# Sine and cosine tables made beside a projection, and a head's two decay spreads in different rows of the array

## What is computed

```python
# S5: 64 groups of 16 channels, 64 complex states each
lam_bar = exp(lam * dt)                    # one complex number per state
bu = einsum('gpc,bsgc->bsgp', b_bar, u_g)
states = scan(s -> lam_bar * s + bu)
y = einsum('gcp,bsgp->bsgc', c_mat, states).real + d * u
# SSD, per head, in chunks of 128 positions
dt = softplus(dt_raw + dt_bias); adt = dt * -exp(a_log)
acs = cumsum(adt)                          # within a chunk
lmat = exp(where(tri, acs[l] - acs[s], -inf))
y = (C B^T * lmat) @ (x * dt) + exp(acs) * (C @ carried_state)
```

## Time and profile before

| | |
|---|---|
| median of 3 runs | 3925.47 us (3924.04 to 3925.93) |
| the profiled execution | 3926.31 us, its span 3924.5 us |
| busy share of the span: PE, PEld, DVE, ACT, POOL | 93%, 73%, 53%, 28%, 28% |
| mean granted PE clock | 0.959 of 2.4 GHz |
| S5 stage | about 692 to 889 us |
| GLU | from 889 us |
| first, second SSD stage | about 2580 to 2641, 3305 to 3364 us |

### The profile page before, as it was taken

The page is one execution under the profiler, slowest core; times in us unless marked ns, Lnnn a source line. Parts: engine busy times, 40 slices in busy tenths (PEclk is TensorE's granted clock), DMA queues, the critical chain, the costliest instruction groups (busy, mean ns, idle before and its releaser), DMA issues. The chain is left out here.

```text
span 3924.5 us, 44371 instructions
## 1 busy us (share of the span) xinstructions
PE 3649.6 (93%) x16819; PEld 2845.9 (73%) x16819; DVE 2065.8 (53%) x2631; ACT 1080.3 (28%) x1480; POOL 1096.8 (28%) x835
## 2 busy tenths in 40 slices
PE   7999999878999979999899999987899999789999
PEld 6767888657788858887667888753688877257887
DVE  4556555894544475454555545655533346554334
ACT  4542221032212122212542221333321223332221
POOL 0635542700645236340544543012100000130000
PEclk9999999889999989999999999987999998899999
DMA  3215443033444334432214443200133321013332
GB/s 105 65 49 135 122 136 105 27 71 93 129 131 135 87 93 135 130 106 83 54 46 123 130 131 104 75 13 22 57 97 103 88 80 45 22 44 86 91 96 81
DMA packets 554319, 346.08 MB, mean 88 GB/s; under 512 B 33270, under 2 KB 535420, under 8 KB 554172
## 3 DMA queue, kind: packets, MB, share of 16 engines
q1 hardware_dynamic: 540348, 293.79, 26.6%
q0 software_dynamic: 13824, 50.34, 4.4%
HBM read 341.01 MB, written 3.08 MB: 88 GB/s over the span
## 5 line engine op out<-in xcount | busy, mean ns | idle before, releaser
L1273 PE MATMUL ps<-h_hi,w_hi 128*128 128x512 f32 x2880 | 1144.6, 397 | 41.6 <-DVE w_lo L1235 14.6
L1274 PE MATMUL ps<-h_lo,w_hi 128*128 128x512 f32 x2880 | 1127.4, 391 | 0.0
L1275 PE MATMUL ps<-h_hi,w_lo 128*128 128x512 f32 x2880 | 1126.2, 391 | 0.0
L1235 DVE TENSOR_TENSOR w_lo<-w,w_hi 128x2048 fp32r<-128x2048 f32 (+2 forms) x294 | 664.3, 2260 | 133.8 <-ACT w_hi L1228 131.7
L1228 ACT ACTIVATE w_hi<-w 128x2048 fp32r<-128x2048 f32 (+2 forms) x294 | 507.0, 1725 | 711.9 <-PE ps L1275 638.1
L1273 PEld LDWEIGHTS ps<-h_hi,w_hi 128*128 128x128 f32 x2880 | 545.1, 189 | 161.9 <-issue 36.1
L1275 PEld LDWEIGHTS ps<-h_hi,w_lo 128*128 128x128 f32 x2880 | 543.9, 189 | 115.2
L1274 PEld LDWEIGHTS ps<-h_lo,w_hi 128*128 128x128 f32 x2880 | 544.8, 189 | 107.9 <-issue 0.5
L1364 DVE TENSOR_TENSOR sg<-sg,ps 128x512 f32<-128x512 f32 x132 | 90.8, 688 | 719.2 <-ACT sg L1349 719.2
L1273 PE MATMUL ps<-a_hi,w_hi 128*128 128x512 f32 x1056 | 411.9, 390 | 0.0
L1275 PE MATMUL ps<-a_hi,w_lo 128*128 128x512 f32 x1056 | 411.0, 389 | 0.0
(11 more groups left out here) (471 smaller groups left out, 3971.6 us busy)
## 6 DMA issues: line engine op xcount, KB each, us to landing
w<-in_ffn_w_gate_up SPq DMA_DIRECT2D x176, 512.0 KB
w<-in_w_ada POOLq DMA_DIRECT2D x96, 512.0 KB, 6.9
w<-in_ffn_w_down SPq DMA_DIRECT2D x64, 704.0 KB
w<-in_w_gate_up SPq DMA_DIRECT2D x88, 512.0 KB
w<-in_w_down SPq DMA_DIRECT2D x32, 704.0 KB
w<-in_fox_w_in SPq DMA_DIRECT2D x32, 512.0 KB
w<-in_w_in SPq DMA_DIRECT2D x14, 1024.0 KB
w<-in_fox_w_in SPq DMA_DIRECT2D x8, 1024.0 KB
```

The lines of the kernel that those rows point to most:

```text
L1235: last = nc.vector.tensor_tensor(lo, raw, hi.bitcast(F32), ALU.subtract)
L1273: nc.tensor.matmul(out, hi, a[0][:, k, :], start=k == 0, stop=False)
L1274: nc.tensor.matmul(out, hi, a[1][:, k, :], start=False, stop=False)
L1275: return nc.tensor.matmul(out, lo, a[0][:, k, :], start=False, stop=k == kt - 1)
```

## The change

It takes the tables out of the S5 stage and puts them, as a side of its own, `S5Tables`, into the second half of layer 0's last projection, spread over chunks 0 to 6; the doubling of the angle after the last table is gone. `ec`, `es` move to arena tiles 8 to 15 and what stood there to 16 to 23. In SSD the small tensors get a second copy of the 8 rows in partitions 32 to 39 (`MR` = 40, which makes the rows between live too); the second spread reads these. `heads` is loaded five times over.

```diff
+MR = 32 + MH
-        self.s5_low = at("s5_low", 16 * S, [P, DK, S], F32R)
+        self.s5_low = at("s5_low", 8 * S, [P, DK, S], F32R)
-        self.heads = sb("heads", [MH, 4])
+        self.heads = sb("heads", [MR, 4])
...
-        self.ut = at(8, 4096).rearrange("p (g a c) -> p g a c", a=4, c=C5)
+        self.ut = at(16, 4096).rearrange("p (g a c) -> p g a c", a=4, c=C5)
...
-        self.ec, self.es = at(16, 2048), at(20, 2048)
+        self.ec, self.es = tables.ec, tables.es
...
         weights(0)
         for q in range(3):
             block(q)
         weights(1)
-        turns()
-        for n in (1, 2, 4, 8):
-            table(n)
         weights(2)
-        table(16)
         block(3)
         block(4)
         block(5)
         keep(0)
-        table(32)
         block(6)
...
+class S5Tables:
+    def __init__(self, m, prep):
+        self.m, self.sm = m, prep.sm
+        flat = m.arena[:, :]
+        self.ec, self.es = (flat[:, t * S:(t + 4) * S] for t in (8, 12))
+        self.etmp = flat[:, 0:1024]
...
+    def vector(self, e, j):
...
+        def cosines(n):
+            t = three(self.etmp[:, 0:32 * n], n)
+            wc, ws = wide(sm["cs"], n), wide(sm["sn"], n)
+            do(tt(ec[:, :, n:2 * n], ec[:, :, 0:n], wc, ALU.mult))
+            do(tt(t, es[:, :, 0:n], ws, ALU.mult))
+            do(tt(ec[:, :, n:2 * n], ec[:, :, n:2 * n], t, ALU.subtract))
...
+        def double():
+            do(tt(sm["t"], sm["cs"], sm["cs"], ALU.mult))
+            do(tt(sm["k"], sm["sn"], sm["sn"], ALU.mult))
+            do(stt(sm["sn"], sm["sn"], 2.0, sm["cs"], ALU.mult, ALU.mult))
+            do(tt(sm["cs"], sm["t"], sm["k"], ALU.subtract))
+        if j == 0:
+            for x in range(3):
+                double()
+                do(tt(sm["er"], sm["er"], sm["er"], ALU.mult))
+            nc.vector.memset(ec[:, :, 0:1], 1.0)
+            do(nc.vector.memset(es[:, :, 0:1], 0.0))
+        for n in {1: (1, 2), 2: (4,), 3: (8,), 4: (16,)}.get(j, ()):
+            cosines(n)
+            sines(n)
+            double()
+        if j == 5:
+            cosines(32)
+        if j == 6:
+            sines(32)
...
                 for i, name in enumerate(("dt_bias_2", "a_log_2")):
-                    e.dma_start(m.heads[0:MH, 2 * l + i:2 * l + i + 1], d[name][l].rearrange("(h a) -> h a", a=1)).then_inc(ld.sem, 16)
+                    for a in range(MR // MH):
+                        e.dma_start(m.heads[a * MH:a * MH + MH, 2 * l + i:2 * l + i + 1], d[name][l].rearrange("(h a) -> h a", a=1)).then_inc(ld.sem, 16)
...
-            mm(ps[:, b, :], m.ones[0:MH, :], self.am[h % 2], start=True, stop=True).then_inc(m.sem["bc_ready"], 1)
-            mm(ps[:, b + 1, :], m.ones[0:MH, :], self.am[h % 2], start=True, stop=False)
+            mm(ps[:, b, :], m.ones[0:MH, :], self.am[h % 2][0:MH], start=True, stop=True).then_inc(m.sem["bc_ready"], 1)
+            mm(ps[:, b + 1, :], m.ones[32:MR, :], self.am[h % 2][32:MR], start=True, stop=False)
...
-            ts(self.am[h % 2], self.acs, m.c("ident")[0:MH, h:h + 1], None, ALU.mult).then_inc(m.sem["am_ready"], 1)
+            ts(self.am[h % 2], self.acs, m.c("sel")[0:MR, h:h + 1], -1.0, ALU.mult, ALU.mult).then_inc(m.sem["am_ready"], 1)
...
-               units=l * 2 * (FH_K + 1), side=prep if l == 0 else None, final=l == 3)
+               units=l * 2 * (FH_K + 1), sides=(prep, tables) if l == 0 else (None, None), final=l == 3)
```

More of the change, by code:

```diff
@@ L731, with __init__ @@
     late = True
-    def __init__(self, m, w, norm, prep):
+    def __init__(self, m, w, norm, prep, tables):
         super().__init__(m)
@@ L740, in __init__ @@
         self.ug = at(0, 4096).rearrange("p (g c) -> p g c", c=S5_CH)
[L741 to L745 removed]
+        self.ut = at(16, 4096).rearrange("p (g a c) -> p g a c", a=4, c=C5)
+        self.y = [at(16 + 2 * i, 1024)[0:S5_CH].rearrange("p (j n) -> p j n", j=S5_L) for i in range(2)]
+        self.st = [[at(20 + i, 256, 256 * a).rearrange("p (r c) -> p r c", r=4) for a in range(2)] for i in range(2)]
+        self.rot = [at(22, 256, 256 * i) for i in range(4)]
+        self.ec, self.es = tables.ec, tables.es
         self.wt = [at(24 + i, S) for i in range(3)]
@@ L1011, in keep @@
             last.then_inc(m.sem["k_ready"], 1)
[L1013 to L1038, removed]
         weights(0)
@@ L1532, in end, with sync, tensor, scalar @@
         finish(self.m, c_loaded=32, s5_loaded=16 * 5, s5_rows=1, turned=1, s5_step=2, s5_act=2, c_turned=2, ct_ready5=2)
+class S5Tables:
[4 more added lines that the diff above has]
+        self.etmp = flat[:, 0:1024]
+    def sync(self, e): pass
+    def tensor(self, e, j): pass
+    def scalar(self, e, j): pass
+    def end(self): pass
+    def vector(self, e, j):
+        m, nc, sm = self.m, self.m.nc, self.sm
+        tt, stt = nc.vector.tensor_tensor, nc.vector.scalar_tensor_tensor
+        do = lambda ins: m.dve(e, ins)
+        three = lambda a, n: a.rearrange("p (i a) -> p i a", a=n)
+        wide = lambda a, n: a.rearrange("p (i a) -> p i a", a=1).broadcast_to([P, 32, n])
+        ec, es = three(self.ec, S5_CH), three(self.es, S5_CH)
+        def cosines(n):
[4 more added lines that the diff above has]
+            do(tt(ec[:, :, n:2 * n], ec[:, :, n:2 * n], t, ALU.subtract))
+        def sines(n):
+            t = three(self.etmp[:, 0:32 * n], n)
+            wc, ws = wide(sm["cs"], n), wide(sm["sn"], n)
+            do(tt(es[:, :, n:2 * n], es[:, :, 0:n], wc, ALU.mult))
+            do(tt(t, ec[:, :, 0:n], ws, ALU.mult))
+            do(tt(es[:, :, n:2 * n], es[:, :, n:2 * n], t, ALU.add))
+        def double():
[17 more added lines that the diff above has]
+            sines(32)
 class SplitDown(Split):
@@ L2417, in vector @@
         self.ahead(e, 1, "vector")
-        nc.vector.tensor_scalar(self.sp.y, m.ps[0:MH, 4, :], m.heads[0:MH, 2 * self.l:2 * self.l + 1], None, ALU.add).then_inc(m.sem["sp_y"], 1)
+        nc.vector.tensor_scalar(self.sp.y, m.ps[0:MR, 4, :], m.heads[0:MR, 2 * self.l:2 * self.l + 1], None, ALU.add).then_inc(m.sem["sp_y"], 1)
         self.ahead(e, 2, "vector")
@@ L2483, in __init__ @@
         self.nacs, self.dec, self.cd = sm[:, 64:96], sm[:, 96:128], sm[:, 128:160]
-        self.na = sm[0:MH, 160:161]
+        self.na = sm[0:MR, 160:161]
     def tensor(self, e):
@@ L2508, in tensor @@
             for c in range(ST):
-                last = tr(ps[:, 0, 32 * i + 8 * c:32 * i + 8 * c + 8], src[:, c * P:(c + 1) * P], ident[0:MH, 0:MH])
+                last = tr(ps[:, 0, 32 * i + 8 * c:32 * i + 8 * c + 8], src[0:MH, c * P:(c + 1) * P], ident[0:MH, 0:MH])
         last.then_inc(m.sem["rows_turned"], 1)
@@ L2566, in scalar @@
         act = nc.scalar.activation
-        act(self.na, m.heads[0:MH, 2 * self.l + 1:2 * self.l + 2], ACT.Exp).then_inc(m.sem["a_ready"], 1)
+        act(self.na, m.heads[0:MR, 2 * self.l + 1:2 * self.l + 2], ACT.Exp).then_inc(m.sem["a_ready"], 1)
         for g in range(2):
@@ L2990, in build, with swiglu @@
             m.resume(ends)
-def swiglu(m, out, gate_up, down, norm, gate=None, units=None, side=None, final=False):
+def swiglu(m, out, gate_up, down, norm, gate=None, units=None, sides=(None, None), final=False):
     parts = []
@@ L2997, in swiglu @@
         ada = AdaUnits(m, units + half * (FH_K + 1), FH_K + 1) if units is not None else None
-        parts += [SplitGateUp(m, gate_up, half, None if half else norm, ada), SplitDown(m, down, half, gate, None if half else side, final)]
+        parts += [SplitGateUp(m, gate_up, half, None if half else norm, ada), SplitDown(m, down, half, gate, sides[half], final)]
     for a, b in zip(parts, parts[1:]):
@@ L3008, in plan @@
     prep = S5Prep(m)
+    tables = S5Tables(m, prep)
     for l in range(4):
@@ L3017, in plan @@
         elif l == 1:
-            s5 = S5Mix(m, d["s5_w_in"][0], PlaceNorm(m, lambda k, l=l: m.col("mix", 8 * l + k)), prep)
+            s5 = S5Mix(m, d["s5_w_in"][0], PlaceNorm(m, lambda k, l=l: m.col("mix", 8 * l + k)), prep, tables)
             glu = SplitGlu(m, d["s5_w_glu"][0])
```

13 lines of the change are left out of this document (6 added, 7 removed).

## The result

The changed kernel took a median of 3874.18 us (4 runs, 3873.01 to 3879.85), the kernel before 3925.70 (4 runs, 3924.04 to 3926.23). The direction was right, the size was not. The profiled execution of the changed kernel is the slowest of its four: span 3878.0, mean granted clock 0.969 (0.959 before).

What follows compares the result with a forecast made beforehand. The prediction took TensorE (PE), busy for 93% of the span, as the bound. Its terms -26.5 + 3.0 + 8 - 16.3 = -31.8, from 3926.3, gave a forecast of 3894 us, range 3883 to 3914.

Steps and rivals of the forecast that it cites:

- Term 1 and 2: Sine and cosine tables: leaving the S5 stage gains 26.5 us; running in the last projection costs 3.0 us.
- Rival C: Tables cost DVE in the projection what they cost in the S5 stage: slower, 3935 us; chance 0.04.
- Term 3: Sixteen more heads transfers in SP's queue ahead of the GLU weights, 0.5 us each: cost 8 us.
- Rival D: Heads transfers cost over 0.8 us each, or table work meets PE's splits worse: 3905 or so; chance 0.05.
- Term 4: SSD stages: a head's two spreads in two row groups overlap in both passes: gain 16.3 us, 8.15 a layer.
- Rival A: SSD spreads: row groups do not overlap because both use all 128 columns: 3910 us; chance 0.24.
- rival B: SSD spreads overlap by one pass only, giving half the row-group term: 3902 us; chance 0.12.

Runs made afterwards that it cites:

- e1: The change with only the tables moved (one row group, 9 transfers), against the kernel before: 3899.55 us, ratio 0.9937.
- e2: The kernel before with only the two row groups for the spreads and the 25 transfers; tables stay in S5: 3899.82 us, ratio 0.9937.
- e3: The change, but the second spread reads the first one's rows 0 to 7, so no overlap: 3905.74 us, ratio 0.9952 to before.
- e7: The change plus 16 unread matmuls in PE's wait ahead of the state products, both SSD stages: 3871.69 us, ratio 0.9874 to before.
- e11: e3 with each spread multiplying all 128 rows, of which 8 count: 3882.73 us, ratio 0.9904 to before.
- e10: e4 with table operations dealt out to fit DVE's free time, plus the 16 matmuls of e7: 3856.13 us, ratio 0.9835 to before.
- e9: The change with the causal mask's matmul (128 rows) placed between the two spreads: 3917.51 us, ratio 0.9987 to before.
- e6: e3 plus 16 unread matmuls in PE's wait ahead of the state products, both SSD stages: 3891.72 us, ratio 0.9923 to before.
- e4: The change with transfers of wdt, heads and dskip moved to the end of the S5 stage's SP queue: 3865.18 us, ratio 0.9848 to before.
- e12: The change with one transfer bringing the 40 rows of a heads column, 9 transfers instead of 25: 3870.72 us, ratio 0.9874 to before.

## Why the prediction was wrong, and where it was right

| term | forecast | measured |
|---|---|---|
| tables out of S5, into the projection | -26.5 + 3.0 = -23.5 | -24.5 (e1) |
| 16 transfers | +8 | +4.3 (PE's wait) |
| row groups, both stages | -16.3 | -28.6 (e2, less the transfers) to -31.5 (the change against e3) |
| sum | -31.8 | -48.8 to -51.7; the change itself -51.5 |

**Term 1 and 2, right in size.** The waits of PE that hung on the tables went, the loop started 26.4 us earlier against the projection's end, the operations cost what the earlier trace rows had for them alone, and PE lost 1.29 and 1.26 us. That the first is so near its forecast of 1.25 is partly luck: the forecast's own prices give 4.6 us of side work at j=1 (14 operations at 0.22 and 6 at 0.26), not 4.9, and so a stall of 0.95. Rival C, the contended price, is excluded by the rows at 647 to 686.

**Term 3, sized too high.** The price of 0.5 us was a choice between two single gaps, 0.34 and 0.78; five in a row take 1.65 to 2.23, and the queue got 5.4 us longer for 16. The low end was the right one. And "PE's wait grows by all of it" did not hold: it grew by 4.3, below the lower bound of 5.4. Together 3.7 us of the miss. Rival D, over 0.8 each, is excluded by the same rows.

**Term 4 is the step that failed.** Its mechanism is right: both passes overlap, a head is 3.05 us for 3.90. Rival A (no overlap) and rival B are excluded by the rows at 2600.37. By the Trainium skill ("TensorE: Matmul & The Clock Gate", Part 3: Packing small matmuls) matmuls start and end in program order. The trace agrees for the matmuls as wholes and not for their passes: the second matmul's first pass starts 0.01 us after the first one's first pass, ahead of that one's second. What failed is the sentence that took the slow stretch of the kernel before as given ("head 3, half in the slow stretch: 1.1; head 2, slow: 1.7"), and with it the bound of 18. The slow stretch came from the form that was removed. Eight heads take 41.5 us in e3 and 31.8 if each runs at full clock (2.23 + 6 x 3.90 + 6.14 for the last head and products); the change takes 27.7, and 26.2 at full clock (e7). So of 13.8 us a stage 5.6 are overlap at full clock, and 8.2 are clock. The forecast had 8.15 in all, and of these 1.1 for the clock (what heads 2 and 3 had above 0.86 each). Its other 7.05 were too much for the overlap: PE's idle time in the heads grew from 0.29 to 1.46 us, which took 1.2 of the 6.9 that sixteen passes less are worth (0.43 each). In the profiled execution of before the heads were shorter (38.2) than in e3 and in the second stage of e1 (41.4, clock 0.75), so between the two profiles only 4.9 of the 10.5 us a stage are clock. The two stages of e1:

```profile
2571.10:2609.30 38.20, 37.91 (x154) 21.73 (x154) 14.44 (x23) 16.12 (x43) 10.20 (x8) 0.82 0.00 1
3287.80:3329.20 41.40, 41.11 (x154) 23.48 (x154) 14.43 (x23) 16.12 (x43) 10.20 (x8) 0.75 0.00 1
```

So one profile can understate what is there to win. The table of engines had the sign of it, too: the last row has PE busy for 48.8 us of 56 at a clock of 0.82, and I didn't ask why.

**What stays open.** Between the profiled executions 46.5 us went, between the medians 51.5. By the heads' rows above, of the 46.5 14.7 went before the first stage's heads, 21.0 in the heads of both stages, 6.7 between them and 4.1 behind. The last two, 10.8 us, are in none of the terms. A part of them is this: in the profile of before the last of the latent attention and the first of its projection ran partly at half clock, in the change not. Before, and after:

```profile
2760.00:2780.00 20.00, 14.90 (x54) 10.03 (x55) 10.21 (x16) 6.94 (x11) 1.56 (x1) 0.66 0.21 65
```

```profile
2732.00:2752.00 20.00, 14.47 (x80) 10.61 (x77) 10.59 (x16) 7.35 (x12) 2.22 (x2) 1.00 0.22 75
```

The profiles of e1 and e3, whose spreads are of the old form, have full clock there, and between and behind the heads they take what the change takes (678.5 and 678.7 us between, 562.5 behind; the change 678.8 and 562.5, before 685.5 and 566.6). So this looks like a matter of one execution and not of the change; single profiles can't settle it. It also means that the 28.6 to 31.5 us of the row groups are covered by rows only in part: 27.5 between e3 and the change, 21.0 between before and the change. The 5 us by which the change's other runs are below its profiled one have no profile. And why the clock falls with few rows, and with how many it would not, was not tried.

## What to carry over

Before a slow stretch of TensorE's clock is booked as a given, look at what PE does in it: here it hung on the very matmuls that the change shortened, so the gain was twice the saved passes. Here two small f32 matmuls that followed one another ran as one in different row groups; where that can't be, zeros in the unused rows cost PE nothing and kept the clock (21.3 us in the heads' rows of e11 against e3). Small transfers are paid by the queue they stand in, so their place decides: ahead of a weight stream PE waited 9 us behind them, at the end of an idle queue not at all.

## What the runs showed of the hardware

- The granted clock fell to half in the middle of unbroken PE work whose spreads used 8 of the 128 rows (e3: idle 0.29 us of 41.5, clock 0.75), and did not with 128 rows (e11: idle 0.31 of 30.8, clock 1.00). PE's last wait had ended 5 us before the heads in both. With two row groups it fell too, for less: 0.94 in the change, 0.83 in one stage of e10, 1.00 in e7.
- Two f32 matmuls of 512 columns in rows 0 to 7 and 32 to 39, into two banks, start 0.01 us apart and run both passes together, although both use all 128 columns; a matmul over all rows between them ends that (e9), and a head is then 0.3 us longer at half clock than with no overlap at all (7.72 for 7.43).
- 16 matmuls in PE's wait took 14 us off the one-group form; off the other 2.5, which is not told from nothing. In single executions of the one-group form the eight heads took from 35.0 (e6) to 46.4 us (e6, its other stage), with the same work.
- A small transfer (8 rows) of the SP queue was issued in 0.33 to 0.45 us in the change (1.65 to 2.23 for five; once 2.58 in e4), one with 40 rows in 0.7 to 0.9 (e12).
